# Last norm's inverse moved behind the MLP, and ScalarE's logarithm/exponential tables loaded by name

## The reference

```python
def _rmsnorm_2(x, w):
    x32 = x.astype(jnp.float32)
    y = x32 * lax.rsqrt(jnp.mean(x32 * x32, axis=-1, keepdims=True) + EPS)
    return (y * w.astype(jnp.float32)).astype(x.dtype)
...
        x = x + jnp.concatenate([o_mla, o_diff], axis=-1) @ w_out[layer]

        h = _rmsnorm_2(x, mlp_norm_w[layer])
        x = x + jnp.square(jax.nn.relu(h @ w_up[layer])) @ w_down[layer]
```

## Time and profile before

| | us |
|---|---|
| median of 3 runs | 3474.01 (3472.73 to 3475.5) |
| the profiled execution, its own time | 3470.08 |
| its span, first to last instruction | 3468.3 |
| TensorE busy (matmuls) | 3196.1 (92% of the span) |
| VectorE busy | 1516.6 (44%) |
| GpSimd busy | 1277.8 (37%) |
| ScalarE busy | 888.1 (26%) |
| mean granted TensorE clock | 0.964 of full speed |

### The profile page before, as it was taken

How to read it: one execution, slowest core, us unless ns; L and a number is a source line. 1 busy time by engine, 2 the same in 40 slices (tenths; PEclk the granted TensorE clock), 3 DMA queues, 4 the chain that set the end, 5 groups by cost and what they waited for, 6 DMA issues and landing times.

```text
span 3468.3 us, 34997 instructions
## 1 busy us (share of the span) xinstructions
PE 3196.1 (92%) x13583; PEld 2489.5 (72%) x13594; DVE 1516.6 (44%) x2274; ACT 888.1 (26%) x1239; POOL 1277.8 (37%) x603
## 2 busy tenths in 40 slices
PE   7999999999688899999997898799788899999999
PEld 5788775588465788888885676487556677878787
DVE  2799946462743422112125301367972322222233
ACT  3322116502333200000002341655563200000000
POOL 2254333244512333333332233454412334444343
PEclk9899999999899999999998999999899999999999
DMA  2022310052100111111110122532120011111111
GB/s 100 31 91 96 129 42 1 1 188 103 61 25 24 37 44 48 48 48 48 48 49 31 45 73 91 163 89 76 45 76 31 30 49 43 48 48 42 48 48 73
DMA packets 66840, 209.14 MB, mean 60 GB/s; under 512 B 7085, under 2 KB 18517, under 8 KB 65977
## 3 DMA queue, kind: packets, MB, share of 16 engines
q1 hardware_dynamic: 39552, 141.31, 12.9%
q10 hardware_dynamic: 27192, 66.54, 5.3%
HBM read 171.11 MB, written 36.46 MB: 60 GB/s over the span
## 4 chain that ended last, share of the span: by engine, by line
PE 81%; DVE 11%; ACT 5%; issue 2%; POOL 1%; ACTq 0%; DMA 0%; DVEq 0%; POOLq 0%
PE ps L514 24%; PE ps L516 24%; PE ps L515 24%; PE ps L552 3%; PE ps L715 2%; DVE x L1631 1%; DVE y L1630 1%; PE ps L1007 1%; DVE rows L1946 1%; DVE rows L1963 1%; PE ps L705 1%; DVE second L1946 1%; PE ps L1019 1%; DVE hidden_lo L1846 1%; DVE hidden_lo L2039 1%
## 5 line engine op out<-in xcount | busy, mean ns | idle before, releaser
L403 POOL TENSOR_TENSOR w_hi<-w_raw,zero 128x1024 fp32r<-128x1024 f32 x210 | 405.7, 1932 | 1742.7 <-PE ps L516 1735.8
L514 PE MATMUL ps<-normed_hi,w_hi 128*128 128x512 f32 x1488 | 589.0, 396 | 42.9 <-DVE normed_lo L1615 29.3
L515 PE MATMUL ps<-normed_lo,w_hi 128*128 128x512 f32 x1488 | 583.7, 392 | 0.0
L516 PE MATMUL ps<-normed_hi,w_lo 128*128 128x512 f32 x1488 | 583.5, 392 | 0.0
L406 POOL TENSOR_TENSOR w_lo<-w_raw,w_hi 128x1024 fp32r<-128x1024 f32 x210 | 557.6, 2655 | 16.5
L514 PE MATMUL ps<-hidden_hi,w_hi 128*128 128x512 f32 x864 | 342.4, 396 | 30.4 <-DVE hidden_lo L2039 18.8
L514 PEld LDWEIGHTS ps<-normed_hi,w_hi 128*128 128x128 f32 x1488 | 282.5, 190 | 108.7 <-issue 34.8
L516 PE MATMUL ps<-hidden_hi,w_lo 128*128 128x512 f32 x864 | 340.6, 394 | 0.0
L515 PE MATMUL ps<-hidden_lo,w_hi 128*128 128x512 f32 x864 | 340.2, 394 | 0.0
L515 PEld LDWEIGHTS ps<-normed_lo,w_hi 128*128 128x128 f32 x1488 | 282.6, 190 | 60.5 <-issue 2.2
L516 PEld LDWEIGHTS ps<-normed_hi,w_lo 128*128 128x128 f32 x1488 | 282.1, 190 | 59.7
(11 more groups left out here) (360 smaller groups left out, 5386.6 us busy)
## 6 DMA issues: line engine op xcount, KB each, us to landing
w_raw<-weights_dram SPq DMA_DIRECT2D x228, 512.0 KB, 3.4
gates_scratch<-tmp ACTq DMA_DIRECT2D x24, 512.0 KB, 2.7
gated<-gates_scratch ACTq DMA_DIRECT2D x24, 512.0 KB, 5.6
head_raw<-diff_qk_scratch SPq DMA_DIRECT2D x32, 256.0 KB, 4.1
x_in<-x_dram ACTq DMA_DIRECT2D x4, 1024.0 KB, 11.0
x<-x_dram ACTq DMA_DIRECT2D x1, 4096.0 KB, 14.1
diff_qk_scratch<-d_out ACTq DMA_DIRECT2D x8, 512.0 KB, 2.6
mla_nope_scratch<-g_nope ACTq DMA_DIRECT2D x8, 512.0 KB, 3.0
```

The source lines that it names most:

```text
L403: nc.gpsimd.tensor_tensor(w_hi[s][:], raw[s][:], zero[:, 0:1].broadcast_to([P, 1024]), ALU.add).then_inc(w_rounded, 1)
L514: nc.tensor.matmul(out, sh, mh, start=start, stop=False)
L515: nc.tensor.matmul(out, sh, ml, start=False, stop=False)
L516: return nc.tensor.matmul(out, sl, mh, start=False, stop=stop)
```

## The change

Two things. First, three calls of `preload_act_table_set("natural_log_exp_and_others")` put a load of the one table set that holds both Ln and Exp at the program's start, behind the sigmoids and behind the SiLUs; the compiler then places no load ahead of a Ln or an Exp. Second, the norm `mlp_2`: `normed` is x times the gain without the inverse, made tile by tile as `out_2` finishes them; the squares are added up on DVE (`add_square`) and summed over the features by PE once, behind `first_tiles`; the inverse is squared (Exp with scale -1.0) and multiplied into the finished MLP sum, which is now kept in `y` apart from x. `out_2` takes turns over four pieces of PSUM in place of two, and its loop is written out.

```diff
@@ block.tensor
-            with pe.Fori(1, 4) as it:
-                for s in range(2):
-                    pe.wait_ge(w_split, 2 * it + s0 + s + 1)
-                    pe.wait_ge(x_added, 2 * it + 3 * KT + s - 1)
-                    tile(s, 0, o_all, KT, s).then_inc(w_used, 1)
-            total("mlp_2")
-
+            for n in range(2, KT):
+                pe.wait_ge(w_split, s0 + n + 1)
+                if n >= 4:
+                    pe.wait_ge(x_added, 3 * KT + n - 3)
+                tile(n % 2, 0, o_all, KT, n % 4).then_inc(w_used, 1)
+
+            pe.wait_ge(x_added, 3 * KT + 6)
             first_tiles("mlp_2", "mlp_2", normed)
+            pe.wait_ge(x_added, 3 * KT + KT)
+            pe.wait_ge(n_acc, 7 * 4)
+            over_features(wide(3), acc, ones[:]).then_inc(n_sum, 1)
...
                 for j in range(first, CHUNK):
                     pe.wait_ge(w_split, 8 * c + s0 + j + 1)
+                    if first and j == 3:
+                        pe.wait_ge(n_rs, 10)
@@ block.scalar
             step = Chain(act, act_step)
+            nc.scalar.preload_act_table_set("natural_log_exp_and_others")
...
                     stage(2 * it + 16 + half, 2 * it + half, ACT.Copy, 1 - half, False)
-
+            nc.scalar.preload_act_table_set("natural_log_exp_and_others")
...
             ffn_hidden(FF_TILES // CHUNK, FF_TILES % CHUNK)
+            nc.scalar.preload_act_table_set("natural_log_exp_and_others")
...
-            squares("mlp_2", lambda k: x[:, k, :], lambda k: (x_added, 3 * KT + k + 1))
-            inverse(9)
-            round_hi("mlp_2", normed[0])
+            before = PRE["mlp_2"][1]
+            for k in range(KT):
+                act.wait_ge(x_added, 3 * KT + k + 1)
+                nc.scalar.activation(normed[0][:, k, :], x[:, k, :], ACT.Copy, scale=col("mlp_2", k)).then_inc(n_hi, 1)
+                post_square(3, k, x[:, k, :])
+            act.wait_ge(n_sum, 10)
+            step(nc.scalar.activation(acc[:], wide(3), ACT.Ln, bias=eps[:], scale=1.0 / D))
+            nc.scalar.activation(acc[:], acc[:], ACT.Exp, scale=-1.0).then_inc(n_rs, 1)
...
-                act.wait_ge(u_added, 8 * (FF2_TILES // CHUNK) + m + 1)
+                act.wait_ge(x_added, 4 * KT + m + 1)
                 act.dma_start(out[:, m, :], x[:, m, :]).then_inc(stored, 16)
@@ block.vector
+            before = PRE["mlp_2"][1]
             for k in range(KT):
                 dve.wait_ge(w_used, SLABS["out_2"][0] + k + 1)
-                tt(x[:, k, :], x[:, k, :], wide(k % 2), ALU.add).then_inc(x_added, 1)
-            scaled(9, "mlp_2", x, normed)
+                tt(x[:, k, :], x[:, k, :], wide(k % 4), ALU.add).then_inc(x_added, 1)
+                if k >= 2:
+                    add_square(3, k - 1)
+                dve.wait_ge(n_hi, before + k + 1)
+                stt(normed[1][:, k, :], x[:, k, :], col("mlp_2", k), normed[0][:, k, :].bitcast(F32), ALU.mult,
+                    ALU.subtract).then_inc(n_lo, 1)
+            add_square(3, KT - 1)
+            nc.vector.memset(y[:], 0.0).then_inc(y_zero, 1)
+            dve.wait_ge(y_zero, 2)
...
-                    tt(x[:, m, :], x[:, m, :], wide(m % 4), ALU.add).then_inc(u_added, 1)
+                    tt(y[:, m, :], y[:, m, :], wide(m % 4), ALU.add).then_inc(u_added, 1)
+                    if last:
+                        dve.wait_ge(u_added, 8 * chunks + m + 1)
+                        dve.wait_ge(n_rs, 10)
+                        step(tt(y[:, m, :], y[:, m, :], acc[:], ALU.mult))
+                        tt(x[:, m, :], x[:, m, :], y[:, m, :], ALU.add).then_inc(x_added, 1)
+
+            with dve.Fori(0, chunks - 1) as c:
+                mlp_hidden(c)
+            mlp_hidden(chunks - 1, True)
```

More of the change, by code:

```diff
@@ L2032, in _, with mlp_hidden @@
             down0 = 4 + 4 + 4 * (FF_TILES // CHUNK) + 6
-            with dve.Fori(0, FF2_TILES // CHUNK) as c:
+            chunks = FF2_TILES // CHUNK
+            def mlp_hidden(c, last=False):
                 for j in range(CHUNK):
```

## The result

| | before | after |
|---|---|---|
| median of four runs each, taken together, us | 3474.6 (3472.7 to 3475.5) | 3432.7 (3427.9 to 3433.7) |
| ratio, 95% interval | | 0.9877 (0.986 to 0.9894) |
| the profiled execution, its own time | 3470.1 | 3433.0 |
| its span | 3468.3 | 3431.2 |

Faster by 41.9 us; the sum said 33.7 and the range began at 3434.0. The direction came as forecast, and so did the mechanism at the places that the prediction named. The size was 8 us short. In the two profiled executions the difference is 37.1, so 3.4 of the 8 are in the traces and 4.8 are not.

A forecast was written before the change was run, and what follows sets the result against it. PE was taken to bound the kernel, four fifths of its chain; seam, stage behind, tail, heads' norms and other loads summed to 33.7 us, so 3474.0 - 33.7 = 3440.3 us, with an 8-in-10 range of 3434 to 3450.

The forecast's parts named there:

- the loads of the two seams: Before the gated MLP and before the second block: two exposed table loads each, 1.3 us apiece, 2.6 per seam gained.
- the MLA heads: End of the MLA heads' loop: without loads DMA issues start at Ln's end and Exp starts earlier; 2.4 us gained (1.3 to 2.8).
- the heads' norms: Ahead of `out_2`: eight loads go, the seventh input tile comes 4.0 us earlier; 4.9 us gained (4.0 to 5.7).
- the seam: From the last `out_2` tile to the MLP's first matmul: the norm leaves the path, POOL's `w_lo` releases PE; 15.7 us gained.
- the stage behind it: Behind `first_tiles`: the sum of squares fills PE's wait for the third slab and a slow start goes; 2.6 us gained.
- the tail: Behind the last matmul: a product and an addition of two SBUF tiles are added on DVE; 2.6 us lost (2.4 to 3.0).
- start and memory stage: Exposed loads at the start and before and in the memory stage go: 2.5 and 1.7 us gained.
- the half of a slow start: At the heads: PE's idle stretch shrinks from 2.73 to about 2.5 us, so half of the 1.7 us half-clock loss was counted gained.
- The rival of loads that cost more than their row: At some 14 exposed loads: each also holds up its neighbours, giving 18 us more gain, 3422 us; chance 3%.
- the value taken: Split of the MLP's second slab beside DVE's square addition: `w_hi` as now, `w_lo` slowed to 3.2 us, PE starting at 2714.7.
- The prediction's objection: On the lock rule for POOL and DVE: POOL's 0.9 us slowdown is less than a whole DVE instruction.
- the exponentials at double time: In the three softmaxes: the common table set slows Exp, at double time the kernel would be near 3510 us; chance 3%.

The follow-up runs named there:

- `norm_only`: Changed kernel without its three named table loads, so Ln and Exp load their sets as before; last norm still applied behind the MLP: 3455.0 us, ratio 0.9961.
- `loads_only`: Kernel before with the three named table loads alone, the last norm staying ahead of the MLP: 3448.6 us, ratio 0.9941.
- `seam_in_turn`: Changed kernel with the last MLP's first two tiles one behind the other instead of interleaved: 3426.0 us, ratio 0.9875.
- `late_by_06`: Changed kernel with one more 512-column copy on ACT between the first sum of squares and its Ln: 3435.9 us.
- `late_by_22`: Changed kernel with two more 1024-column copies on ACT between the first sum of squares and its Ln: 3435.5 us.
- `all_three_late`: Changed kernel with paired down tiles, last MLP's first tiles in turn, folded tail, plus a 512-column ACT copy at the start: 3382.7 us.
- `all_three`: Changed kernel with paired down tiles, last MLP's first two tiles in turn, and x + y r² formed ahead of the last down tiles: 3380.9 us, ratio 0.9744.
- `loads_back`: Changed kernel with the load between Ln and Exp put back in four norms, before the gated MLP and before the second block: 3438.9 us.

## Why the prediction was wrong

Two steps failed. First, the sum charged the loads of the two seams at their rows alone (2.6 and 2.6) and put nothing for the products behind the differential norms and for the last MLP's chunks. In the profiles these gave 4.6, 3.2, 1.3 and 1.5: together 5.4 more, of which the MLA heads and the heads' norms took 2.0 back. Second, it carried the difference from one profile to the median of three runs; the medians of four lie 4.8 further apart than the profiles. Where those 4.8 come from stays open. The numbered points below take this up.

Right: the seam (15.7 against 15.5, with 5.5 us to PE's start, `w_hi` 1.89, `w_lo` 3.20 and the slab as releaser), the stage behind it (2.6 against 2.7), the tail (-2.6 against -2.5), start and memory stage within 0.1, the heads' norms within 0.7 (their path gave the 4.0, but the half of a slow start did not come: one wait of 1.99 is left of the three where I expected 2.5, and it is followed by seven matmuls at half clock, which the like wait of 1.96 before was not). The start's agreement is in part luck: the third tile of the first projection begins at 60.5 to 62.2 in the three profiles without the named load and at 58.6 to 60.3 in the eight with it and without an added copy, 1.5 apart on average. Loads at the price of their row: the loads alone gave 21.3 in all. The rival of loads that cost more than their row falls with `norm_only` and `loads_only`, and so does the rule of the Trainium skill that went with it ("ScalarE: Activation LUTs", section "What ACT_TABLE_LOAD costs"): at 2.66 a load, four put back would have cost 10.6 in their seams; the profile has 6.2, of which 5.2 are the rows'. The softmaxes are no slower: attention took 0.4 less.

The rule on the lock of the port, in the Trainium skill, "SBUF — State Buffer", section "SBUF: two separate sides", was told as the value taken: `w_hi` as alone, `w_lo` late. The trace agrees, down to the single instruction. DVE's addition of the square began at 2690.70, inside `w_hi`, and ended at 2692.6, 1.1 behind `w_hi`'s end. `w_lo`, begun at 2691.57, ended at 2694.8, 2.2 behind the addition. `normed_lo`, begun at 2692.50, ended at 2695.9, 1.1 behind `w_lo`. So each waited out the other's instruction and then took its own time (1.23, 2.34 and 1.28) less 0.1 to 0.2. All 143 DVE instructions of 1024 columns with two SBUF inputs that in after's trace begin inside a slab's split end 1.1 behind it, and so do the 126 in before; an addition from PSUM beside `w_hi` took its 1.22 (2689.56). The prediction's objection, that POOL loses 0.9 us and not a whole DVE instruction, misreads this: POOL waits only for what is left of DVE's.

One estimate among the rivals was worked out wrongly: with the exponentials at double time, 96 x 1.06 more, the forecast of 3440 becomes about 3542, not 3510.

Wrong:

1. *"And carry the difference over to the median of the runs."* The three runs shown, 3472.7 to 3475.5, are at the upper end of what before does: 44 later runs of it, in four sets, have medians of 3469.5 to 3470.0 and reach from 3466.4 to 3475.7. With both kernels at their later medians the gain is 39 to 40. But at the recorded 3432.7 after was itself 3 above its later median, so this is no simple offset; and a forecast of a time needed a wider range for both ends than "the scatter of runs (about 1.5)" gave it.
2. *The clock outside the named places.* The sum had slow starts at the third MLP tile and half of one at the heads. The first pair of profiles has some 5 us of gain more of this kind: 1.6 at the total over `acc`, 0.4 and 0.6 in the seams, 1.3 behind the differential norms, 1.5 in the last MLP's chunks. The 1.3 repeats in every profile (48.2 us for that stage with the loads, 46.9 without). The 1.6 is 1.4 and 0.6 in the other two profiles with the loads. The 1.5 is one slow start, four in before and three in after; `seam_in_turn`, without the loads, has four. The slow starts of before were there to be read: after each wait I could have taken the granted clock. Which of them would go was not to be read from it.
3. *The early stretch*, which comes in two values 6.7 us apart. It was long in all three profiles without the named load at the start (before twice, `norm_only`), and short in five of the eleven with it. That the load moved by the change favours the short one is suggested by this count and not shown. `late_by_06` and `late_by_22` lie all high, so something under a microsecond at the start may take it away; but `all_three_late`, with the same copy, has a run at 3379.3 with the clock (0.975) of the short ones, and its median is only 1.8 above that of `all_three`. If the short stretch came in five of eleven runs of after and in none of before, that would be 3.0 on average: an estimate from these counts, and not a measured share.
4. On the other side the MLA heads gave 1.1 of 2.4 in the first pair. But the first profile of before was quick there: the stage is 90.3, 93.8 and 93.6 in the three profiles with its loads and 87.5 to 89.9 in the eleven without, 3.4 apart on average. So one pair of profiles can't give this term; the 2.4 lies between that pair's 1.1 and this 3.4.

## What to carry to other kernels

Once the named path is worked out row by row, list every wait of the bottleneck engine with the granted clock behind it, and allow for the slow start as well as the wait: here up to 1.6 us for each, also at waits that the change did not touch. Put it into the range and not only into the sum, since the length of a wait does not tell whether it comes. Take the range from the scatter of executions, which a median of three hides. And where the bottleneck engine waits for the last of several inputs at the same place in every turn of a loop, give it the first inputs of a second output to work on: that one reordering brought 34.5 us, nearly as much as the whole change.

## What the runs showed of the hardware

- After waits of equal length (2.34 us) in equal chunks TensorE's granted clock falls to 1.2 GHz for some 8 matmuls behind some and behind others not. The distances of the chunks were 91.3, 91.3, 89.7, 91.3, 89.7, 91.3, 89.7 in both profiles of before; in after they were 89.7, 89.7, 91.3, 89.7, 91.3, 91.3, 89.7 and then 89.7, 89.7, 91.3, 91.3, 89.7, 91.3, 89.7. The number of long ones repeated, their places not always.
- Behind a norm's idle stretch the first two tiles had about 12 matmuls at 1.2 GHz and the third none, or about 7 and again about 7. Both came behind a stretch of 7.3 us (`norm_only`, `loads_back`) and both behind one of 6.05 (after, `all_three`).
- A DVE instruction with two SBUF inputs that begins inside one of POOL's splits ended 1.1 us behind it in all 269 cases of two traces, and POOL's instruction in turn ended 1.7 to 2.3 behind DVE's. The two took turns; one from PSUM ran beside it in its own time.
- A stretch of 40 us in which PE is busy over nine tenths of the time (37.9 to 39.7 of 40) can have a mean clock of 0.62 or of 0.83 in the same program, and 0.6 us more on ACT at the start of after went with a median 4.5 us higher (the same copy in `all_three`, 1.8).
- A table set named once served Ln, Exp, Square, Copy and ReLU without a further load and without a change of their times (Ln 1.11 to 1.12, Exp 1.06).
